# Two-layer encoder step in split fp32: the seven-product form for the first layer's FFN input as well, with the modulation sums and the output weights' low parts on VectorE in the output stages

## The reference, cut to what matters

```python
for i in range(DEPTH):                                   # DEPTH = 2
    sh1, sc1, gt1, sh2, sc2, gt2 = jnp.split(cs @ w_ada[i] + b_ada[i], 6, axis=-1)
    h = ada_modulate(rms_norm(x, g_mix[i]), sh1, sc1)
    o = mixer_i(h)                                       # sparse attention, then forgetting attention
    x = x + gt1[:, None, :] * o
    h = ada_modulate(rms_norm(x, g_ffn[i]), sh2, sc2)
    gate, up = split_cols(h @ w_ffn_in[i], (D_FF, D_FF)) # D_MODEL 1024, D_FF 2816
    x = x + gt2[:, None, :] * ((silu(gate) * up) @ w_ffn_out[i])
shf, scf = jnp.split(cs @ w_ada_final + b_ada_final, 2, axis=-1)
y = ada_modulate(rms_norm(x, g_final), shf, scf)
```

## Time and profile before

| | |
|---|---|
| median of 3 runs | 1649.82 us (1648.64 to 1658.67) |
| the profiled execution | 1651.07 us, its span 1648.6 us |
| granted clock, mean | 0.977 |
| busy, share of the span | PE 95%, DVE 54%, POOL 43%, ACT 35% |
| chain that ended last | PE 86%, issue 5%, ACT 4%, DVE 2%, POOL 2% |
| PE lines on it | L722 53% (units), L1223 13% (products), L739 4% |
| FFN 0, from its third unit to output B's last two units | 409.85 to 809.57 |
| the same of FFN 1 | 1249.59 to 1608.66 |

### The profile page before, as it was taken

The page is one execution under the profiler, slowest core; times in us unless marked ns, Lnnn a source line. Parts: engine busy times, 40 slices in busy tenths (PEclk is TensorE's granted clock), DMA queues, the critical chain, the costliest instruction groups (busy, mean ns, idle before and its releaser), DMA issues.

```text
span 1648.6 us, 29657 instructions
## 1 busy us (share of the span) xinstructions
PE 1564.8 (95%) x11750; PEld 1425.7 (86%) x11750; DVE 890.1 (54%) x1734; ACT 585.2 (35%) x1132; POOL 705.5 (43%) x343
## 2 busy tenths in 40 slices
PE   5898899899999999999988999999899999999997
PEld 3667865598999999999977888888799999999997
DVE  2558845515665645556683344434439871388503
ACT  2434245424222112222253334334335542255424
POOL 2213751153555345546622222222444764466551
PEclk9799999899999999999999999999899999999998
DMA  8675420023555453554424333332131343033321
GB/s 284 198 273 184 107 52 2 1 64 110 159 163 180 156 160 124 171 181 153 114 63 112 97 109 113 97 103 77 39 101 53 103 126 101 29 92 103 97 70 58
DMA packets 240971, 188.83 MB, mean 115 GB/s; under 512 B 12504, under 2 KB 228224, under 8 KB 233584
## 3 DMA queue, kind: packets, MB, share of 16 engines
q1 hardware_dynamic: 228720, 181.49, 36.7%
q10 hardware_dynamic: 12160, 6.09, 1.2%
HBM read 175.44 MB, written 8.50 MB: 112 GB/s over the span
## 4 chain that ended last, share of the span: by engine, by line
PE 86%; issue 5%; ACT 4%; DVE 2%; POOL 2%; POOLq 0%; SPq 0%; DMA 0%; ACTq 0%; DVEq 0%
PE lin L722 53%; PE lin L1223 13%; PE lin L739 4%; PE S L982 2%; PE O L1031 1%; PE O L805 1%; PE O L1100 1%; PE T L1011 1%; PE S L874 1%; ACT act_hi L1426 1%; PE S L1053 1%; POOL ssq L1921 1%; PE S L917 1%; POOL w_lo L1901 1%; PE T L1068 1%
## 5 line engine op out<-in xcount | busy, mean ns | idle before, releaser
L1901 POOL TENSOR_TENSOR w_lo<-w_raw,w_hi 128x1024 fp32r<-128x1024 f32 (+2 forms) x148 | 434.6, 2938 | 624.1 <-ACT w_hi L1377 624.0
L722 PE MATMUL lin<-act_hi,w_hi 128*128 128x288 f32 (+1 forms) x1696 | 255.3, 303 | 11.4 <-ACT act_hi L1405 5.3
L722 PE MATMUL lin<-act_hi,w_lo 128*128 128x288 f32 (+1 forms) x1696 | 255.3, 299 | 4.7 <-POOL w_lo L1901 4.5
L722 PEld LDWEIGHTS lin<-act_hi,w_hi 128*128 128x128 f32 (+1 forms) x1696 | 236.3, 192 | 23.6 <-issue 16.1
L722 PE MATMUL lin<-act_lo,w_hi 128*128 128x288 f32 (+1 forms) x1696 | 248.6, 297 | 0.0
L722 PEld LDWEIGHTS lin<-act_hi,w_lo 128*128 128x128 f32 (+1 forms) x1696 | 235.2, 190 | 11.9 <-issue 6.3
L722 PEld LDWEIGHTS lin<-act_lo,w_hi 128*128 128x128 f32 (+1 forms) x1696 | 233.1, 188 | 3.8 <-issue 3.5
L1377 ACT ACTIVATE w_hi<-w_raw 128x1024 fp32r<-128x1024 f32 (+2 forms) x148 | 164.8, 1114 | 172.3 <-PE lin L722 118.0
L2426 DVE SCALAR_TENSOR_TENSOR acc<-ada_raw,cs_w,acc 128x2048 f32<-128x2048 f32 x56 | 182.4, 3298 | 0.0
L2360 DVE SCALAR_TENSOR_TENSOR x<-lin,mods,x 128x512 f32<-128x512 f32 (+1 forms) x80 | 37.7, 512 | 203.4 <-PE lin L722 203.4
L2037 POOL TENSOR_TENSOR w_lo<-ada_raw,w_hi 128x512 fp32r<-128x512 f32 x57 | 78.9, 1387 | 65.0 <-ACT w_hi L1667 65.0
(11 more groups left out here) (313 smaller groups left out, 2496.3 us busy)
## 6 DMA issues: line engine op xcount, KB each, us to landing
ada_raw<-in_w_ada SPq DMA_DIRECT2D x36, 1024.0 KB, 6.3
w_raw<-in_w_ffn_in SPq DMA_DIRECT2D x50, 512.0 KB, 4.1
w_raw<-in_w_ffn_out SPq DMA_DIRECT2D x32, 704.0 KB, 6.1
ada_raw<-in_w_ffn_in SPq DMA_DIRECT2D x38, 512.0 KB, 5.2
w_raw<-in_w_in_b SPq DMA_DIRECT2D x32, 512.0 KB, 4.1
w_raw<-in_w_in_a SPq DMA_DIRECT2D x16, 512.0 KB, 5.7
ada_qo<-in_w_ada SPq DMA_DIRECT2D x8, 1024.0 KB, 7.2
ada_raw<-in_w_ada_final SPq DMA_DIRECT2D x8, 1024.0 KB, 5.0
```

Source lines behind the costliest of these rows:

```text
L722: last = nc.tensor.matmul(lin_u(u)[0:m, tok], w, (lo if p == 2 else hi)[:, at(t) if at else t, tok], start=(p == 0 and t == 0), stop=(p == ...
L1901: TT(w_lo[:, u % 2, 0:n], w_raw[:, u % 2, 0:n], w_hi[:, u % 2, 0:n].bitcast(F32), ALU.subtract)\
```

## The change

The parts:
1. FFN 0's input gets FFN 1's form: 3 plain tiles and 19 pairs (8 in half A, 11 in half B). The functions of FFN 1 take a layer number; the ring and the PSUM banks swap places by the parity of the layer's first unit.
2. `ada_sums` goes. In its place stand 64 steps `half_sum(k)` of 1024 columns (two operations each), in 8 blocks of 8 steps. They run only in output stages, two steps per unit, on DVE between the low part of the next unit and the residual of this one: 5 units of attention output 0, 7 of FFN 0 output A, 6 of FFN 0 output B, 6 of attention output 1, 8 of FFN 1 output A. Each loads 512 KB.
3. Each half block is collected (`sum_collect`, 8 matmuls) and transposed (`sum_transpose`) on PE. The collection stands behind the unit whose steps finish the block: unit 3 of attention output 0, units 2 and 6 of FFN 0 output A, 3 of FFN 0 output B, 1 and 5 of attention output 1, 3 of FFN 1 output A; the last one behind unit 0 of FFN 1 output B.
4. The low parts of all output units but each stage's first are made on DVE (`wlo_vec`), not on POOL.
5. The second half of `ada_raw` is shared by pairs of odd number and the sums, so SP's loads of either wait for the other.

```diff
+SUM_OA, SUM_F0A, SUM_F0B, SUM_OB, SUM_F1A = 0, 5, 12, 18, 24
+OUT_UNITS = [u0 + m for u0 in (U_OA, U_OB, *U_OUT) for m in range(1, KT)]
@@ SP
+            def out_stage_loads(u0, w, kt, sums, first_sum, between=None, pairs=0):
+                users = [p for p in range(pairs) if raw_slot(p) == 1]
+                for m in range(KT):
+                    w_load(u0 + m, w[:, m * P:(m + 1) * P], kt, P)
+                    if between is not None:
+                        between(m)
+                    if m == 2 and users and sums:
+                        sp.wait_ge(ws_lo_p, pool_lo(users[-1], W_A22))
+                    if m >= 2 and m - 2 < sums:
+                        sum_loads(first_sum + m - 2)
+                for m in range(KT - 2, sums):
+                    sum_loads(first_sum + m)
@@ PE
+            def sum_collect(hb):
+                pe.wait_ge(ada_acc, 16 * (hb + 1))
+                pe.wait_ge(ada_row_done, 3 + hb)
+                for s in range(2):
+                    for j in range(2):
+                        last = nc.tensor.matmul(O[32 * j:32 * j + 32, 0:512], pick[:, s, :],
+                                                acc[:, s, 512 * j:512 * j + 512], start=(s == 0), stop=(s == 1))
+                last.then_inc(ada_used, 1)
+            def out_stage(u0, kt, ready, hi, lo, collect, nz=None, rest=None, pairs=0, at=None):
+                for m in range(KT if nz is None else KT - 2):
...
+                    if m - 1 in collect:
+                        lin_part(u0 + m, None, kt, P, hi, lo, ready=have, some=some[:kt], at=at)
+                        sum_transpose(collect[m - 1])
+                        some = some[kt:]
+                    lin_part(u0 + m, None, kt, P, hi, lo, ready=have, some=some, at=at)
+                    if m in collect:
+                        sum_collect(collect[m])
-            ffn_half(U_F0, 1, ACT_N1, 0, None, lambda: ada_collect(3), after_first)
-            ffn_half(U_F0 + FFN_N, None, None, HT, begin_second, lambda: ada_collect(5), after_second,
-                     lambda: ada_collect(6), 2)
+            out_stage(U_OA, KT, ((ohi_done, 0), (olo_done, 0)), act_hi, act_lo, {3: 0}, 1)
+            ffn_stage(0, 1, ACT_N1, {2: 1, 6: 2}, {3: 3})
...
+            out_stage(U_OB, KT, split_ready(ACT_OB), act_hi, act_lo, {1: 4, 5: 5}, 3, [(p, KT - 1) for p in range(3)])
+            ffn_stage(1, 3, ACT_N3, {3: 6}, {0: 7})
@@ ACT
+            def out_stage(u0, n, n_next, collect, nz=None):
+                for m in range(KT - 1):
+                    split_hi(u0 + m + 1, n)
+                    if m - 1 in collect:
+                        sum_evac(collect[m - 1])
+                    if nz is not None and m < KT - 2:
+                        act.wait_ge(lin_free[(u0 + m) % 2], free_count(u0 + m))
+                        square(nz, m)
@@ DVE
+            def half_sum(k):
+                hb, kt = k // 8, k % 8
+                dve.wait_ge(sum_in[k % 2], 16 * (k // 2 + 1))
...
+                for e in range(2):
+                    if kt == 0:
+                        V.tensor_scalar(acc[:, e, :], sum_raw(k), cs_w[:, 0, e:e + 1], None, ALU.mult).then_inc(ada_acc, 1)
+                    else:
+                        dve.wait_ge(ada_acc, 2 * k - 1 + e)
+                        V.scalar_tensor_tensor(acc[:, e, :], sum_raw(k), cs_w[:, kt, e:e + 1], acc[:, e, :],
+                                               ALU.mult, ALU.add).then_inc(ada_acc, 1)
+            def split_lo(u, n):
+                dve.wait_ge(whi_done, u + 1)
+                V.tensor_tensor(w_lo[:, u % 2, 0:n], w_raw[:, u % 2, 0:n], w_hi[:, u % 2, 0:n].bitcast(F32), ALU.subtract)\
+                    .then_inc(wlo_vec, 1)
+            def out_stage(u0, n, gate, collect, sums=0, first_sum=0, nz=None, last=None):
+                for m in range(KT if nz is None else KT - 2):
+                    if m + 1 < KT:
+                        split_lo(u0 + m + 1, n)
+                    if m < sums:
+                        half_sum(2 * (first_sum + m))
+                        half_sum(2 * (first_sum + m) + 1)
+                    if m - 1 in collect:
+                        sum_mods(collect[m - 1])
...
+                    residual_tile(u0, gate, m)
+                if nz is not None:
+                    split_lo(u0 + KT - 1, n)
```

More of the change, by code:

```diff
@@ L61 @@
 U_F0 = U_OA + KT
-FFN_N = 2 * HT + KT
-U_FG = U_F0 + 2 * FFN_N
+FULL = 3
+U_F0B = U_F0 + 2 * FULL + KT
+U_FG = U_F0B + KT
 U_B = U_FG + 1
@@ L95, in last_use @@
 def last_use(q):
-    first = 0 if q < 7 * N_A else 7 * N_A
-    uses = [p for p in range(first, q) if SLOTS[p] == SLOTS[q]]
+    uses = [p for p in range(7 * FIRST[half_of(q // 7)], q) if SLOTS[p] == SLOTS[q]]
     return uses[-1] if uses else None
@@ L645, in _ @@
                             kv_cache_load(r, pair, it, 4 * (PAIRS + r) + 4)
[L646 to L683, removed]
+            out_stage_loads(U_OB, i["w_out_b"][0], KT, 6, SUM_OB)
+            ffn_loads(1)
             for j in range(10):
@@ L1124, in _ @@
             pe.wait_ge(o_free, PAIRS)
[L1126 to L1129, removed]
-                    lin_part(u0 + r, None, kt, P, hi, lo, ready=ready if r == 0 else None, some=rest if r == 0 else None, at=at)
-                    if after is not None:
-                        after(r)
-                with pe.Fori(0, KT // 2 - (1 if nz is None else 2)) as it:
-                    for r in range(2):
-                        linear(u0 + 2 + r, kt, P, it, 2, None, hi, lo, at)
-                if late is not None:
-                    late()
-                if nz is not None:
-                    last_units(u0 + KT - 2, kt, hi, lo, nz)
@@ L1141, in ffn_half @@
-            def ffn_half(u0, nz, act_base, hid_base, begin, middle, after, late=None, nz_out=None):
-                if nz is not None:
-                    first_units(u0, P, nz, act_base)
-                else:
-                    begin(0)
-                    linear(u0)
-                    begin(1)
-                    linear(u0 + 1)
-                with pe.Fori(0, HT - 1) as it:
-                    for g in range(2):
-                        linear(u0 + 2 + g, it=it, per=2)
-                middle()
-                out_linear(u0 + 2 * HT, HT, ((hid_ready, hid_base),) * 2, hid_hi, hid_lo, after=after, nz=nz_out,
-                           late=late)
@@ L1980, in _, with out_stage @@
                 split_pair(pair)
-            def out_stage(u0, n, n_next, nz=None):
-                def tile(r, it, per, cols, more=True):
-                    if more:
-                        split_lo(u0 + r + 1, cols, it, per)
-                    if nz is not None and r < KT - 2:
-                        sum_square(nz, r, it, per)
-                if nz == 4:
-                    pool.wait_ge(sp_done, 7 * N_ALL)
+            def out_stage(u0, n_next, nz=None, pairs=0):
+                if pairs and nz is not None:
+                    pool.wait_ge(sp_done, 7 * pairs)
@@ L2363, in residual_tile @@
                 last.then_inc(lin_free[u % 2], 1)
-            def residual(u0, gate, count=KT):
-                with dve.Fori(0, count // 2) as it:
-                    for r in range(2):
-                        residual_tile(u0, gate, r, it, 2)
             def residual_half(u0, gate, nz, m, h):
```

785 lines of the change are left out of this document (391 added, 394 removed).

## The result

The changed kernel takes **1663.58 us** (median of 13 runs, 1660.86 to 1671.3) against 1649.82 for the kernel before: ratio **1.0083, 95% interval 1.0066 to 1.0100**, 13.8 us slower. Forecast: 1668, range 1634 to 1682. The prediction took 1% as the least that can be told from no change; the interval of these runs is narrower, and by it 0.8% is clear of no change. The profiled execution took 1667.3 us, 16.2 more than the one of before (its span 1665.2 us, 16.6 more), and its differences are read against that.

A forecast was written before the change was run, and what follows sets the result against it. The prediction took TensorE's matmul order and its waits as the bound. Its terms summed to +11.0 us, +17.0 with the clock, on 1651.07 us: 1668.1, or 1666.8 on the runs' median; it said 1668, range 1634 to 1682.

The forecast's parts named there:

- waits, attention output 0: Attention output 0: PE idles 9.4 us at the collection behind unit 3, waiting for DVE's sums; stage +10.4 us.
- period, attention outputs; output B: DVE's turn, residual to residual: 9.4 us in attention outputs against PE's 6.39, 9.8 in FFN 0 output B against 8.8.
- eight half blocks: Output stages: each half block costs PE 2.45 us, 1.8 for collection and 0.65 for transposition.
- clock: TensorE: four idle stretches of 7.5 to 9.4 us each bring 1.2 GHz back once, 1.6 us each, +6 in all.
- FFN 0's input: FFN 0's input: 19 pairs of 84 matmuls in place of 96, at FFN 1's measured cost, save 40.6 us.
- -40.6 + 0.4 + 6.6 + 10.6: FFN 0, in us: input in FFN 1's form, activation sums needed ahead, output A's extra, output B's extra.
- The mechanism: Output stages: PE waits 7 to 10 us ahead of `sum_collect` in four places, each ended by DVE's sum.
- the term of 0.5: DVE's turn in attention outputs: POOL's addition of squares and DVE take turns on the SBUF port, +0.5 us per period.
- the +17.0 of the sum: Whole kernel: all terms add to +11.0 us, with the clock +17.0, on the profiled execution's 1651.07 us.
- A: Output stages: DVE's turn fits PE's unit, so no collection waits; -27 us, 1624 us; chance 0.15.
- B: Output stages: more lead, one of two collections per block met; idle 18 us, clock 3, about 1646 us; chance 0.13.
- C: Half blocks' second loads land late, each turn grows 1 to 2 us in 15 turns; 1685 us; chance 0.10.

The follow-up runs named there:

- experiments 1 and 3: Against the changed kernel: 1, most sums in stages with a norm cut to 64 of 1024 columns, 1625.05 us; 3, residual before sums, loads one unit earlier, 1641.39 us.
- Experiment 5: Output weights' low parts back on POOL: in the changed kernel 1703.24 us; in the kernel with residual first and the sums dealt out anew 1662.47 us.
- experiment 6: Changed kernel with residual ahead of sums, loads a unit earlier, and the 32 turns of sums dealt out anew over the stages: 1632.29 us, ratio 0.9899.
- experiment 7: Kernel of experiment 6 with attention output 0's waiting collection moved behind the first third of the next unit, its transposition behind the second: 1632.51 us.

## Why the prediction was right

| step | predicted | measured |
|---|---|---|
| waits, attention output 0 | 9.4 | 7.80 |
| attention output 1 | 8.8, 9.4 | 8.18, 7.88 |
| FFN 0 output A, B | 1.7, 7.7 | 0.77, 4.56 |
| period, attention outputs; output B | 9.4; 9.8 | 8.93; 9.36 |
| eight half blocks | 2.45 each | 1.84 + 0.39 = 2.23 each |
| clock | 4 x 1.6 = 6 | 8.9, range 5 to 13; by the rows 8.7 |
| FFN 0 as FFN 1, without what is put in | -40.6 | PE without a gap in both product stages |

**FFN 0's input** held. The stretch that the prediction measured begins in the third unit, at its second third; in the changed kernel that is

```profile
424.40 2.40 PE L784 MATMUL lin<-act_hi,w_lo 128*128 128x288 f32 x16
```

and from there to output B's unit 6 it takes 799.22 - 424.40 = 374.8 us, 24.9 less than before. The prediction's terms for that stretch, -40.6 + 0.4 + 6.6 + 10.6, less the 0.5 that lies behind unit 6, and 1.6 of clock give -21.9. That is 3.0 us too little. The shorter waits would give 4.1 and the cheaper half blocks 0.7, together 4.8; some 1.8 us the other way I can't place.

**The mechanism** held: the places named for 7 to 10 us have waits of 7.8, 8.2 and 7.9, the fourth only 4.6, below the 7 that was to show it; all are ended by DVE's sums, and experiments 1 and 3 show that the sums and their place in the order make them; in FFN 0 output B the late first loads have a part in it.

**The sizes** were off twice, in opposite directions. *The period* was 0.45 too long. The square starts 0.97 us behind the residual's start, not 1.21: the 1.21 was read at residual 0 of the earlier trace rows. The addition of squares lengthens the low part by 0.4, the term of 0.5. The waits follow: three periods 0.45 too long are 1.4 of the 1.6 us at attention output 0. In output B the first turn was cheaper as well: it opens a half block, whose two first operations take 1.42 us together and not 2.4, which I had not counted; residual 0 comes at 749.23 - 737.02 = 12.2 instead of 13.8.

*The clock* was too cheap. I took the price of one slow stretch from the earlier trace rows; behind these waits the collection lost 1.7 us (3.63 for 1.91) and the matmuls behind it up to 0.9 (3.32 for 2.40), 1.7 to 2.6 in all and not 1.6. The Trainium skill, TensorE: Matmul & The Clock Gate, "Part 1: The HAM clock gate", has the clock halve after idleness; the runs agree, 0.50 behind the waits and 1.00 with PE kept busy through them, 1.0083 against 1.0029.

Part of it cancels: waits 29.2 for 37.0, half blocks 1.8 less, clock 3 more, together 6.6 below the +17.0 of the sum, so +10.4. The profiled executions differ by 16.2, of which 2.3 arise ahead of anything changed; the 3.5 us left aren't explained. Some 1.4 of them lie in FFN 0 (the 1.8 above less the dearer clock), and 1.5 in FFN 1, which from its third unit to output B's unit 6 takes 365.1 us for 359.1, with 4.5 for two half blocks. The mechanism carries the forecast; that 1668 lies within 4.4 us of the median is partly luck.

**The rivals.** A (sums hidden, 1624 us) is wrong for this order; the run that shortened the sums came to 1625, so its price was near, and the better order shows how near it was: 1632. B: both collections of attention output 1 waited. C: sums waited for loads at the start of the FFN outputs (3.4, 3.3 and 3.9 us; the two of FFN 0 were counted) and twice within FFN 0 output A (1.0 and 2.1), which I had not counted, but not turn after turn.

**The port.** The Trainium skill, SBUF — State Buffer, "SBUF: two separate sides", has a DVE operation with two SBUF inputs and a GpSimd operation take turns. The prediction used it for one term of 0.5. The runs agree: four sums took 4.87 us with POOL's addition all but gone, 6.04 with it (1.43 us when alone), and 8.1 with a low part on POOL as well. It mattered far more for a thing that the prediction costed at 6 us in all: the low parts' move to DVE, which removes POOL's subtractions from beside the sums. Experiment 5 prices it at 29 and 39 us. I had compared with the waits of the kernel before, where no sums ran in the attention outputs.

## What to carry to other kernels

Where work is put on an engine that is busy half the time, write down one turn of it as a chain: if the new work stands ahead of what another engine waits for, its length is added to the round trip, and idle time in the middle stays unused. Put what others wait for first (here the residual) and the filler behind it, with its loads asked for a turn earlier: the same instructions took 1641 us instead of 1664. Then deal the filler out by the slack per unit of each stage, and price waits of TensorE as long as these (4.6 to 8.2 us) with some 2 us on top for the clock (1.7 to 2.6 here).

## What the runs showed of the hardware

- One two-input operation of POOL (1.43 us) lengthens DVE's series of two-input operations by 1.2 us (6.04 against 4.87); where it meets DVE's idle time only the tail of it counts (0.4).
- The granted clock fell to 0.50 (1.2 GHz) during the wait of 7.8 us and stayed there through the collection and on into the matmuls behind it; with PE kept busy through the same wait it was 1.00 (2.4 GHz) throughout. Four waits, 28 us in all, cost about 9 us more than their length.
- The length of one wait alone doesn't tell: behind a wait of 2.29 us the collection took its 1.91 us (experiment 6), behind one of 1.94 us the clock was 0.50 for a while (experiment 7). Why is open.
- A queue in order can raise a price: the low parts on POOL cost 29 us where the sums' loads were issued a unit earlier (DVE waited 4.8 us for `in_w_ada`), and 39 where they stood behind a load that waits for those low parts (30.7 us). DVE's order differed between the two as well, so the 10 us aren't the queue's alone.
